# The odd layer's convolution: one of VectorE's two channel blocks computed on GpSimd

## The reference, cut to what matters

```
def conformer_conv(p_d, dw_w, dw_b, cn_g, cn_b):
    h = p_d[..., :D_D] * jax.nn.sigmoid(p_d[..., D_D:])     # D_D = 512 channels
    h = causal_dwconv(h, dw_w) + dw_b                       # 31 taps over positions
    h = layer_norm(h, cn_g, cn_b)
    return jax.nn.silu(h)

y_c = forgetting_attention(q, k, v, log_f).reshape(bsz, s, D_C)
y_d = conformer_conv(...)
return jnp.concatenate([y_c, y_d], axis=-1) @ w_out
```

## Time and profile before

| | us |
|---|---|
| median of 3 runs | 1162.05 |
| lowest and highest run | 1161.86, 1162.26 |
| the profiled execution's own time | 1161.88 |
| its span in the profile | 1160.1 |
| TensorE busy in it | 1147.4 |
| VectorE busy | 779.3 |
| ScalarE busy | 604.6 |
| GpSimd busy | 46.5 |

### The profile page before, as it was taken

One profiled execution on the slowest core, in us unless ns is written; L12 is line 12 of the kernel. 1 busy time (PEld: TensorE's weight loads), 2 busy tenths in 40 slices (PEclk: granted clock), 3 DMA queues, 4 the chain that ended last, 5 costly groups with the idle time before them and its releaser, 6 DMA issues.

```text
span 1160.1 us, 18219 instructions
## 1 busy us (share of the span) xinstructions
PE 1147.4 (99%) x6746; PEld 938.9 (81%) x6746; DVE 779.3 (67%) x1149; ACT 604.6 (52%) x896; POOL 46.5 (4%) x82
## 2 busy tenths in 40 slices
PE   8999999999999999999999999999999999999998
PEld 6887888888868888888778888888887778888886
DVE  5798666548897865554778777566466877865641
ACT  5555544425964554443556665445356666654530
POOL 0200000000001000000100100000010011000000
PEclk9999999999999999999999999999999999999999
DMA  9756876745734687664575169777548514877650
GB/s 328 252 169 195 277 217 217 218 147 180 254 93 145 203 271 218 217 208 158 166 238 155 33 195 296 218 214 224 163 147 272 164 56 145 275 222 219 211 171 36
DMA packets 186440, 225.82 MB, mean 195 GB/s; under 512 B 15954, under 2 KB 130298, under 8 KB 186369
## 3 DMA queue, kind: packets, MB, share of 16 engines
q1 hardware_dynamic: 181184, 213.07, 58.2%
q10 hardware_dynamic: 4896, 11.58, 3.1%
q0 software_dynamic: 288, 0.23, 0.1%
HBM read 212.22 MB, written 1.06 MB: 184 GB/s over the span
## 4 chain that ended last, share of the span: by engine, by line
PE 49%; DVE 2%; issue 0%; ACT 0%; POOL 0%; POOLq 0%; DVEq 0%; ACTq 0%
PE ps L601 15%; PE ps L603 14%; PE ps L602 14%; DVE w_lo L1602 1%; PE ps L973 1%; PE ps L769 1%; PE ps L1056 1%; PE ps L1031 1%; PE ps L777 0%; PE ps L1003 0%; PE ps L784 0%; PE ps L1023 0%; PE ps L1020 0%; DVE nbuf L1922 0%; PE ps L1002 0%
## 5 line engine op out<-in xcount | busy, mean ns | idle before, releaser
L1602 DVE TENSOR_TENSOR w_lo<-raw,w_hi 128x1024 fp32r<-128x1024 f32 x377 | 445.4, 1216 | 122.2 <-ACT w_hi L1201 119.1
L1201 ACT ACTIVATE w_hi<-raw 128x1024 fp32r<-128x1024 f32 x377 | 383.3, 1056 | 153.0 <-DMA raw<-w_down 35.2
L601 PE MATMUL ps<-w_hi,a_hi 128*128 128x512 f32 x1039 | 409.1, 394 | 2.2 <-DVE w_lo L1602 1.1
L603 PE MATMUL ps<-w_hi,a_lo 128*128 128x512 f32 x1039 | 404.8, 390 | 0.0
L602 PE MATMUL ps<-w_lo,a_hi 128*128 128x512 f32 x1039 | 404.5, 389 | 0.0
L601 PEld LDWEIGHTS ps<-w_hi,a_hi 128*128 128x128 f32 x1039 | 195.0, 188 | 44.7 <-DVE w_lo L1602 2.1
L603 PEld LDWEIGHTS ps<-w_hi,a_lo 128*128 128x128 f32 x1039 | 195.0, 188 | 41.2
L602 PEld LDWEIGHTS ps<-w_lo,a_hi 128*128 128x128 f32 x1039 | 195.2, 188 | 39.1
L601 PE MATMUL ps<-w_hi,h_hi 128*128 128x512 f32 x480 | 188.3, 392 | 0.5 <-DVE h_lo L2092 0.4
L603 PE MATMUL ps<-w_hi,h_lo 128*128 128x512 f32 x480 | 186.9, 389 | 0.0
L602 PE MATMUL ps<-w_lo,h_hi 128*128 128x512 f32 x480 | 186.9, 389 | 0.0
(11 more groups left out here) (224 smaller groups left out, 675.7 us busy)
## 6 DMA issues: line engine op xcount, KB each, us to landing
raw<-ffn_w_in SPq DMA_DIRECT2D x176, 256.0 KB, 4.1
raw<-w_in SPq DMA_DIRECT2D x96, 256.0 KB, 3.7
raw<-ffn_w_out SPq DMA_DIRECT2D x88, 256.0 KB, 3.1
raw<-w_gate SPq DMA_DIRECT2D x88, 256.0 KB, 3.3
raw<-w_up SPq DMA_DIRECT2D x88, 256.0 KB, 4.0
raw<-w_down SPq DMA_DIRECT2D x88, 256.0 KB, 3.2
moved<-turned SPq DMA_DIRECT2D x176, 64.0 KB, 2.6
raw<-od_w_in SPq DMA_DIRECT2D x40, 256.0 KB, 3.8
```

Source lines behind the costliest of these rows:

```text
L601: nc.tensor.matmul(ps[:, bank, :], hi, wh, start=first, stop=False)
L603: return nc.tensor.matmul(ps[:, bank, :], lo, wh, start=False, stop=last)
L1201: nc.scalar.activation(w_hi[:, v.slot, :], raw[:, v.slot, :], ACT.Copy).then_inc(w_high, 1)
L1602: V.tensor_tensor(w_lo[:, v.slot, :], raw[:, v.slot, :], w_hi[:, v.slot, :].bitcast(F32), ALU.subtract).then_inc(w_low, 1)
```

## The change

Block 1 leaves VectorE's list of taps, which holds only the 31 taps of block 0, and the numbers of taps in the hand-written order become 6, 4 x 1, 4 x 2, 2, and 3 for each pair of heads. GpSimd gets a function `convolve()` at the head of its odd layer's program. It waits for `o_pad` and, on a semaphore `o_edge_set` of its own, for the memset of its edge. For eight taps at a time (8, 8, 8 and 7) it multiplies the eight shifted views of `o_pad` by their weights in one instruction, into a new tile `o_prod` of 8 x 256 columns, then adds the upper half of the products to the lower until one is left (4, 2, 1; for seven 3, 2, 1), then copies it to `o_acc[1]` or adds it to it. Every step waits for the one before. At the end it adds the channel's bias and signals `o_conv2`, for which TensorE waits before `turn_conv(0)`.

```diff
--- before.py
+++ after.py
@@ -82,6 +82,7 @@
 N_W = 12
 HALVED = 3
 LOOP = 3
+AT_ONCE = 8
 
 
 MOVE_AFTER = {3: NC - 4, 7: NC - 3, 11: NC - 2, 13: NC - 1}
@@ -209,6 +210,7 @@
 
         turned, _ = place("turned", [P, LOOP, 4, 2, NT, 32], F32)
         moved, _ = place("moved", [P, LOOP, 4, 2 * NT, 32], F32)
+        o_prod, _ = place("o_prod", [P, AT_ONCE, SEQ], F32)
         assert top[0] <= nc.SBUF_PARTITION_SIZE_BYTES, top[0]
 
 
@@ -391,9 +393,9 @@
         cum_kept, cum_spread = sem("cum_kept"), sem("cum_spread")
         o_built, o_edged, o_quad = stage("o_built", 2, [1]), stage("o_edged", 2, [1]), stage("o_quad", 8, [1])
         o_tapped, o_fourth = stage("o_tapped", 2, [1]), stage("o_fourth", 2, [1])
-        quads_in = sem("quads_in")
+        quads_in, o_edge_set = sem("quads_in"), sem("o_edge_set")
         moved_in = [sem(f"moved_in{r}") for r in range(LOOP)]
-        o_conv, o_back, o_spread, o_scaled = stage("o_conv", 1, [1]), stage("o_back", NT, [1]), stage("o_spread", NT, [1]), stage("o_scaled", NT, [1])
+        o_conv, o_conv2, o_back, o_spread, o_scaled = stage("o_conv", 1, [1]), stage("o_conv2", 1, [1]), stage("o_back", NT, [1]), stage("o_spread", NT, [1]), stage("o_scaled", NT, [1])
         o_normed, o_silu = stage("o_normed", NT, [1]), stage("o_silu", NT, [1])
 
         roped = stage("roped", 1, hyb)
@@ -885,6 +887,7 @@
             def odd_rest():
                 attention(1)
                 pe.wait_ge(o_conv.sem, o_conv.at(1, 0))
+                pe.wait_ge(o_conv2.sem, o_conv2.at(1, 0))
                 pe.wait_ge(o_fourth.sem, o_fourth.at(1, 1))
                 turn_conv(0)
                 turn_y(1, shared, 0)
@@ -1797,7 +1800,7 @@
                 V.tensor_tensor(tiny_lo[:, :, :], tiny_raw[:, :, 0:GATES], tiny_hi[:, :, :].bitcast(F32), ALU.subtract).then_inc(tiny_done, 1)
 
 
-            taps = [(k, b) for k in range(TAPS) for b in range(2)]
+            taps = [(k, 0) for k in range(TAPS)]
             tap_step = {}
 
             def convolve(n):
@@ -1859,21 +1862,21 @@
                     V.tensor_tensor_scan(o_f[:, 1, :], ones, o_f[:, 0, :], 0.0, ALU.mult, ALU.add).then_inc(o_fcum.sem, 1)
                     dve.wait_ge(o_turned.sem, o_turned.at(1, 0))
                     dve.wait_ge(o_gated.sem, o_gated.at(1, 2))
-                    chain.step(V.memset(o_pad[:, :, 0:PADT], 0.0))
-                    chain.settle()
+                    V.memset(o_pad[:, :, 0:PADT], 0.0).then_inc(o_edge_set, 1)
+                    dve.wait_ge(o_edge_set, 1)
                     edges(0)
                     dve.wait_ge(o_padded.sem, o_padded.at(1, 0))
                     dve.wait_ge(o_turned.sem, o_turned.at(1, 1))
-                    convolve(12)
+                    convolve(6)
                     for _ in range(4):
                         feed(fed[0] + 1)
-                        convolve(2)
+                        convolve(1)
                 if c == 2:
                     for _ in range(4):
-                        convolve(3)
+                        convolve(2)
                         feed(fed[0] + 1)
                 if c == 3:
-                    convolve(4)
+                    convolve(2)
                     dve.wait_ge(cum_spread, 16)
                     causal = const[:, C_CAUSAL:C_CAUSAL + P].unsqueeze(1).broadcast_to([P, HEADS, P])
                     chain.step(V.tensor_tensor(o_bias[:, :, 0:P], o_bias[:, :, P:2 * P], causal, ALU.add))
@@ -1885,7 +1888,7 @@
                     chain.settle()
 
             def odd_rest():
-                attention(1, lambda j: convolve(7))
+                attention(1, lambda j: convolve(3))
                 share(1)
                 for t in range(NT):
                     dve.wait_ge(o_back.sem, o_back.at(1, t))
@@ -2224,8 +2227,35 @@
                         pool.wait_ge(spread2.sem, spread2.at(k, t))
                         root(rstd2[:, one], ssq2[:, one], 1.0 / D, RMS_EPS, scaled2, 1)
 
+            def convolve():
+
+                pool.wait_ge(o_padded.sem, o_padded.at(1, 0))
+                pool.wait_ge(o_edge_set, 1)
+                for k in range(0, TAPS, AT_ONCE):
+                    n = min(AT_ONCE, TAPS - k)
+                    edge = o_pad[:, 1, k:k + SEQ]
+                    row = [list(d) for d in edge.ap]
+                    near = bass.AP(tensor=edge.tensor, offset=edge.offset, ap=[row[0], [1, n], [1, SEQ]])
+                    each = pcol[:, 1, R_DW + k:R_DW + k + n].unsqueeze(2).broadcast_to([P, n, SEQ])
+                    chain.step(nc.gpsimd.tensor_tensor(o_prod[:, 0:n, :], near, each, ALU.mult))
+                    chain.settle()
+                    while n > 1:
+                        more = n // 2
+                        chain.step(nc.gpsimd.tensor_tensor(o_prod[:, 0:more, :], o_prod[:, 0:more, :], o_prod[:, n - more:n, :], ALU.add))
+                        chain.settle()
+                        n -= more
+                    if k:
+                        chain.step(nc.gpsimd.tensor_tensor(o_acc[1][:, :], o_acc[1][:, :], o_prod[:, 0, :], ALU.add))
+                    else:
+                        pool.wait_ge(o_turned.sem, o_turned.at(1, 1))
+                        chain.step(nc.gpsimd.tensor_copy(o_acc[1][:, :], o_prod[:, 0, :]))
+                    chain.settle()
+                nc.gpsimd.tensor_scalar(o_acc[1][:, :], o_acc[1][:, :], pcol[:, 1, R_DWB:R_DWB + 1], None,
+                                        ALU.add).then_inc(o_conv2.sem, 1)
+
             for l in every:
                 if LAYERS[l] == "odd":
+                    convolve()
                     for t in range(NT):
                         pool.wait_ge(o_spread.sem, o_spread.at(l, t))
                         root(c_rstd[:, t:t + 1], c_mv[:, t, 1:2], 1.0, LN_EPS, o_scaled, 1)
```

## The result

The changed kernel takes 1185.37 us (median of 5, 1184.63 to 1185.94), the kernel before beside it 1161.86: 1.020 times as long, with a 95% interval of 1.0188 to 1.0211. The profiled execution has a span of 1182.8 us, 22.7 longer than before.

A forecast was written before the change was run, and what follows sets the result against it. TensorE was taken as the bound. turn_conv would come 20 us later (path alone) to 30 (turns, less 1.5 in attention); the middle, 25, on 1160.1 gives 1185.1 span, plus 1.8 around it and 0.17 to the median: 1187, range 1164 to 1206.

The forecast's parts named there:

- the turns: GpSimd's 21 instructions alternate with VectorE's first 21 two-input ones: GpSimd ends at 348.4, first minimum 360.5, turn_conv 30 us later.
- What bounds the kernel: TensorE, busy 1147.4 of 1160.1 us: the kernel gains only where TensorE idles and loses where something makes it wait.
- The path that excludes: In the odd layer's stretch, GpSimd and VectorE's instructions with two SBUF inputs exclude each other, in both directions.
- GpSimd's price per column: GpSimd's convolution: 2.2 ns per two-input column, bounds 1.11 and 3.3, so 40.9 us alone.
- products near 4.7 us: Sign in the after profile: GpSimd's products take near 4.7 us where nothing holds them.
- The hold: GpSimd's convolution occupies the path shared with VectorE's two-input instructions for 39.0 us.
- Attention: With 15 taps fewer on VectorE, first minimum to turn_conv gains 1.5 us (floor 0.8, ceiling 5.9): 15.4 instead of 16.9.
- VectorE not held: Rival: GpSimd waits to start, then both engines run; the 1.5 us gain stays, 1160.5 us; chance 0.07.
- GpSimd always giving way: Rival: GpSimd yields even mid-instruction, ends near 363.5, TensorE waits for o_conv2 alone: 18 us longer, 1180; chance 0.10.
- A price of 1.11 or 3.3: Two rivals on GpSimd's ns per column: 1.11 gives about 1170 us, chance 0.10; 3.3 gives about 1204, chance 0.08.
- Costs that cancel: Rival: little holding and a slow GpSimd that ends just behind 345.76: 1162 us; chance 0.05.
- The tap chain's cost: On VectorE, with one block each tap waits for its neighbour: 0.52 us per tap, 0.12 more.

The follow-up runs named there:

- write_only: The change with GpSimd's instructions replaced by memsets, products and sums twice each, block 1 not computed and block 0's sum transposed twice: 1160.77 us.
- one_input: The change with GpSimd's products and sums made TENSOR_SCALAR with one SBUF input and the same columns, block 1's values wrong: 1176.39 us.
- late: The change with GpSimd's convolution started only behind the first pair's minima on VectorE: 1183.46 us.
- spin: The change with 44 matmuls on constants between TensorE's first taps and the second pair's logits, keeping TensorE busy in its wait: 1183.28 us.
- one_block: The change without GpSimd's convolution and TensorE's wait for it; VectorE keeps 31 taps, block 0's sum is transposed twice: 1160.74 us.

## Why the prediction was right, step by step

The forecast was 1187 and the measured time is 1185.37, in the range and on the side that had 0.88. The mechanism is shown. The sum was 2.3 us too long in the span. That it came so near is in part luck: the turns, which the prediction held likelier and which did happen, were summed to 30 us, and the middle with an end that did not happen made 25 of them.

**What bounds the kernel.** Right: the whole difference is TensorE's wait in this one stretch. 22.0 of 22.7 us arise before the first minimum.

**The path that excludes.** Right, also in the direction that no row of before showed: VectorE is held by GpSimd (3.42 and 4.63 us for a split of 1.22). It is reading that does it, of one input too (write_only, one_input). What is held is VectorE's instructions with two SBUF inputs, and the TENSOR_SCALAR of the last section; its minima (late) and its memsets (0.85 for four at 296.53, as before) are not. The Trainium skill's page (SBUF — State Buffer, Who interferes with whom) has it that a two-input instruction contends with a GpSimd instruction that reads and not with one that only writes; the runs agree, 1185.37 against 1160.77. That GpSimd holds VectorE for its whole instruction, as the prediction had it, fits the two-input products and sums here, and not the TENSOR_SCALAR of 3.44 us, in whose last part a tap took 0.48.

**GpSimd's price per column.** 2.2 ns taken, bounds 1.11 and 3.3. The sums cost (2416 - 190)/1024 = 2.2 (the mean of three in late), the products (3610 - 190)/2048 = 1.67. So alone it needs 36.9 us, as late shows, and not 40.9. The prediction's own sign, products near 4.7 us, did not come true: they take 3.61. The estimate of 2.10 from the Trainium skill's figure (GPSIMD Engine Reference, Performance versus the Vector engine) is near that of the sums, and too much for the products. The bound of 1.7 ns for one input was wrong, it is 2.6: instructions of one and four columns did not give the price of a thousand.

**The hold.** 39.0 us was forecast, 27.0 measured. The price takes 4.0 off: 36.9 instead of 40.9. The other 8 us are the step of the sum that was mis-sized: turns of whole instructions without overlap. By such turns GpSimd's 36.9 us and the 20 two-input instructions that VectorE did meanwhile (14 taps and 6 splits, 12.4 us) need 49.3 us, and both were done in 42.2. Two rows of the change show where it went, GpSimd's sum of 512 columns behind a tap and behind a split:

```profile
302.76 1.35 POOL L2244 TENSOR_TENSOR o_prod<-o_prod 128x512 f32<-128x512 f32 x1
...
311.91 2.15 POOL L2244 TENSOR_TENSOR o_prod<-o_prod 128x512 f32<-128x512 f32 x1
```

With VectorE idle the same sum takes 1.26 (late, at 361.80). So a tap, counted as 0.40, delays GpSimd by 0.1: it mostly fits between two GpSimd instructions. A split, counted as 1.14, delays it by 0.9. GpSimd lost 5.3 us to VectorE (42.2 - 36.9), where 12.8 were forecast. The first 0.8 us held nothing either, as VectorE did its memsets then, until 297.44.

**Turns.** Right that they take turns. GpSimd is done first, at 338.78 instead of 348.4: 2.1 us from its length and 7.5 from the overlap. Behind it VectorE catches up its splits in 12.1 us, as forecast, so the first minimum comes at 350.89 instead of 360.5. With attention 2.2 us longer than was taken, turn_conv is at 368.50. It lies between the two ends of 365.6 and 375.9; their middle was taken, 25 us later than before, and it is 22.7.

**Attention.** A gain of 1.5 us was counted. Without GpSimd it is 16.90 - (344.55 - 328.32) = 0.7, near the floor of 0.8. In the change it became a loss of 0.7, as the clock at 1.2 GHz costs 1.6 (17.6 against 16.0 in spin). I had taken nothing for the clock and named it, with up to 8 us; it stayed at half for 4 us of attention.

**The rivals.** VectorE not held: out, by every row. GpSimd always giving way: out; in late it gave way to almost nothing. A price of 1.11 or 3.3: out. Costs that cancel: out, as GpSimd was done 30 us before it was needed and held VectorE for 27. The tap chain's cost: 0.52 instead of 0.40 per tap (five in 2.57 us in one_block), as forecast, and free, since VectorE has slack.

## What to carry to other kernels

Before moving an elementwise step from VectorE to an idle GpSimd, list what VectorE does meanwhile with two SBUF inputs: here those instructions waited while GpSimd read, so the step wasn't moved but added, at more than twice its price (27 us of hold for 12.3 us of taps). Small GpSimd instructions already in a trace hint at it: the same instruction at 0.19 and at 1.28 us. What ran beside each other without loss here were GpSimd's memsets beside taps and splits, and VectorE's minima, with one input in PSUM, beside GpSimd's products.

## What the runs showed of the hardware that I had not expected

A TENSOR_SCALAR on VectorE with one SBUF input was held as well: 2.92 us beside a product and 1.09 beside a memset of 1.81, against 0.41. I had counted it as free. It waited for the whole GpSimd instruction each time: in one_input for 4.74 us, until 301.98, just behind the product's end at 301.84, though taps and splits got through such products early. On GpSimd a TENSOR_SCALAR with one input costs 2.6 ns per column, more than a TENSOR_TENSOR whose second input is one weight repeated (1.67) or two plain tiles (2.2).
